# Two sparse-attention stages of a four-layer stack: values as the still operand, output by channel, compressed heads in pairs, spatial weights laid out transposed, a new order of weight pieces

## What is computed

```python
def _nsa(q, k_cmp, v_cmp, k_sel, v_sel, k_win, v_win, gates, pe, w1, w2):
    kc = compress(k_cmp, 0)              # 15 compressed keys and values of 64 channels, 2 groups
    vc = compress(v_cmp, 1)
    p_c = jax.nn.softmax(jnp.where(m_c, s_c, NEG), axis=-1) * m_c
    o_cmp = jnp.einsum('bsghn,bngd->bsghd', p_c.astype(vc.dtype), vc)
    ...                                  # selected branch and window branch: 8 heads, causal
    o = g[..., 0:1] * o_cmp + g[..., 1:2] * o_sel + g[..., 2:3] * o_win

def _gmlp(uv, ln_g, ln_b, ws, bs):
    u, v = jnp.split(jax.nn.gelu(uv), 2, axis=-1)
    v = _layernorm(v, ln_g, ln_b)
    w = ws * jnp.tril(jnp.ones((GM_CHUNK, GM_CHUNK), ws.dtype))
    sv = jnp.einsum('gts,bnsgc->bntgc', w, v) + bs.T[None, None, :, :, None]
    return u * sv.reshape(B, S, GM_WIDTH)

merged = jax.nn.sigmoid(zga) * (y_a @ proj_a[l]) + jax.nn.sigmoid(zgb) * (y_b @ proj_b[l])
h = h + mod[:, 1, 2] * (merged @ w_out[l])
```

## Time and profile before

| | |
|---|---|
| median of 3 runs | 2371.98 us (2371.92 to 2376.93) |
| profiled execution | 2374.35 us, span 2372.5 us, mean granted clock 0.968 |
| PE busy | 2234.7 us (94%) |
| DVE, ACT busy | 1627.3 us (69%), 1067.6 us (45%) |
| first and second sparse stage | about 1340 to 1559 us and 1955 to 2173 us of the span |

### The profile page before, as it was taken

How to read it: one execution, slowest core, us unless ns; L and a number is a source line. 1 busy time by engine, 2 the same in 40 slices (tenths; PEclk the granted TensorE clock), 3 DMA queues, 4 the chain that set the end, 5 groups by cost and what they waited for, 6 DMA issues and landing times.

```text
span 2372.5 us, 29998 instructions
## 1 busy us (share of the span) xinstructions
PE 2234.7 (94%) x10820; PEld 1862.0 (78%) x10820; DVE 1627.3 (69%) x2271; ACT 1067.6 (45%) x1271; POOL 0.2 (0%) x4
## 2 busy tenths in 40 slices
PE   3999999999999987999999998999999999899998
PEld 3887887888788766788788887778878888777887
DVE  5777777877777776776777754577677776447445
ACT  3434524444444554434534545454353455454434
POOL 0000000000000000000000000000000000000000
PEclk9999999999999997999999987899999999789999
DMA  7888524788688442786688642368759875134553
GB/s 307 322 325 291 206 88 160 284 318 316 237 319 314 142 151 98 269 306 246 242 317 318 219 149 73 107 225 329 260 205 335 316 253 188 64 105 139 183 209 125
DMA packets 128374, 537.29 MB, mean 226 GB/s; under 512 B 15040, under 2 KB 15904, under 8 KB 109344
## 3 DMA queue, kind: packets, MB, share of 16 engines
q1 hardware_dynamic: 128288, 536.12, 62.2%
HBM read 534.96 MB, written 1.10 MB: 226 GB/s over the span
## 4 chain that ended last, share of the span: by engine, by line
PE 83%; DVE 9%; ACT 5%; DMA 1%; issue 1%; SPq 0%; ACTq 0%; DVEq 0%
PE GU L1588 14%; PE GU L1592 13%; PE GU L1590 13%; PE PY L1588 11%; PE PY L1592 11%; PE PY L1590 10%; DVE wL L900 3%; ACT wH L513 2%; PE TM L1632 1%; ACT M L565 1%; PE GU L2085 1%; ACT xH L560 1%; PE PY L1995 1%; DMA M<-in_ada_t 1%; PE PY L1898 1%
## 5 line engine op out<-in xcount | busy, mean ns | idle before, releaser
L900 DVE TENSOR_TENSOR wL<-raw,wH 128x2048 fp32r<-128x2048 f32 x344 | 776.8, 2279 | 281.6 <-ACT wH L513 280.0
L513 ACT ACTIVATE wH<-raw 128x2048 fp32r<-128x2048 f32 x344 | 645.5, 1901 | 214.6 <-PE PY L1592 128.9
L1588 PE MATMUL GU<-wH,xH 128*128 128x512 f32 (+1 forms) x1584 | 630.1, 398 | 38.8 <-DVE xL L1024 30.7
L1592 PE MATMUL GU<-wH,xL 128*128 128x512 f32 (+1 forms) x1584 | 617.9, 390 | 0.0
L1590 PE MATMUL GU<-wL,xH 128*128 128x512 f32 (+1 forms) x1584 | 617.1, 390 | 0.0
L1588 PEld LDWEIGHTS GU<-wH,xH 128*128 128x128 f32 x1584 | 299.4, 189 | 106.5 <-issue 27.6
L1592 PEld LDWEIGHTS GU<-wH,xL 128*128 128x128 f32 x1584 | 299.2, 189 | 63.2
L1590 PEld LDWEIGHTS GU<-wL,xH 128*128 128x128 f32 x1584 | 300.0, 189 | 57.6
L913 DVE CUSTOM_DVE_ANT_0 ada<-ada,cond 128x1024 f32<-128x1024 f32 x272 | 316.6, 1221 | 0.0
L593 ACT ACTIVATE hH<-TM 128x512 fp32r<-128x512 f32 x80 | 47.9, 598 | 580.5 <-PE TM L1632 580.5
L1588 PE MATMUL PY<-wH,hH 128*128 128x512 f32 x640 | 198.6, 391 | 0.9 <-DVE wL L900 0.9
(11 more groups left out here) (284 smaller groups left out, 1999.8 us busy)
## 6 DMA issues: line engine op xcount, KB each, us to landing
raw<-in_up_w SPq DMA_DIRECT2D x352, 512.0 KB, 6.3
ada<-in_ada_t SPq DMA_DIRECT2D x136, 1024.0 KB, 7.6
raw<-in_down_w SPq DMA_DIRECT2D x176, 512.0 KB, 5.0
raw<-in_c_w SPq DMA_DIRECT2D x96, 512.0 KB, 4.4
raw<-in_a_w SPq DMA_DIRECT2D x40, 512.0 KB, 4.4
raw<-in_b_w SPq DMA_DIRECT2D x32, 512.0 KB, 4.4
M<-in_ada_t SPq DMA_DIRECT2D x8, 1024.0 KB, 12.4
gB<-gates SPq DMA_DIRECT2D x12, 512.0 KB, 5.6
```

The costliest lines, as they stand in the source:

```text
L513: act.activation(wH[:, to, 0:words], raw[:, slot, 0:words], ACT.Copy).then_inc(s_high, 1)
L900: dve.tensor_tensor(wL[:, to, 0:words], raw[:, slot, 0:words], wH[:, to, 0:words], ALU.subtract).then_inc(s_split, 1)
L1588: pe.matmul(outs[i], aH, wh[i], start=first, stop=False)
L1592: ins = pe.matmul(outs[i], aL, wh[i], start=False, stop=last)
```

## The change

The spatial weights come from the host with the summed token on the partitions, so PE no longer turns them, and both token tiles go through one product: 8 products of 128 columns (L2052) for 16 of 64. Compressed probabilities of two heads stand side by side, 32 columns apart (`pcs`), and are turned together (8 turns of 47 rows, L2059). The compressed values of a group stand twice in `vcb`, on the diagonal, so that one product of 512 columns (L2071) serves four heads and both tiles: 2 products for 16. In the maps the values are the still operand (64 columns) and the probabilities of two heads the moving one (256 columns): 2 products (tile 0) or 4 (tile 1) for 4 or 8 (L2105). The two of a pair write partitions 0 to 63 and 64 to 127 of one bank. The output thus stands by channel, and the turn of `yo_` falls away. The second projection's pieces (18 and 19) now come first, 18 stands in front of the values of map 7; they need the spatial result and not the attention's. `w_out`'s pieces come in the other order of halves. The compressed softmax runs ahead of piece 10 on PE and ahead of piece 12's cut on DVE. Three memsets are new at the start. SP's order is the same.

```diff
@@ pieces
-            + [(k0, C_IN + h * 512, 512) for h in range(2) for k0 in (0, 4)]
-            + [(k0, C_OUT + h * 512, 512) for k0 in (0, 4) for h in range(2)])
+            + [(k0, C_IN + h * 512, 512) for k0 in (4, 0) for h in (1, 0)]
+            + [(k0, C_OUT + h * 512, 512) for k0 in (4, 0) for h in range(2)])
@@ build
+        hcv = sb("hcv", [P, 2, 64])
+        vcb = sb("vcb", [P, 2, P])
+        pcs = sb("pcs", [P, NT * 4 * 64])
@@ scalar, nsa
                 evacuate(u_, GU[:, :, :], ACT.Gelu_apprx_tanh)
-                turned(wsT, TMf)
-                cut()
-                cut()
-                turned(yT, PBf)
+                cut()
                 act.wait_ge(s_cx, t.next(s_cx))
                 act.activation(pcf, pcf, ACT.Exp).then_inc(s_ce, 1)
                 exponentials(0, P)
-                evacuate(sg_[0][:, :, 0:512], PY[:, 0:2, :], ACT.Sigmoid)
-                cut()
-                for i in range(NT):
-                    turned(xn[0:NCMP, i, :], TMf[0:NCMP])
...
+                cut()
+                turned(xn[0:32 + NCMP, 0, :], TMf[0:32 + NCMP])
+                turned(yT, GUf)
...
+                    if u == 6:
+                        act.wait_ge(s_eaten, t.next("done", 2))
+                        act.activation(xH[:, 4:8, :].rearrange("p d s -> p (d s)"), yT, ACT.Copy).then_inc(s_xh, 1)
+                        act.activation(gates_out[u], PY[:, 0:2, :], ACT.Sigmoid).then_inc(s_readA, 1)
...
-                high_out(xH[:, 0:4, :].rearrange("p d s -> p (d s)"), PBf)
...
+                act.wait_ge(s_o, t.next(s_o, 2))
+                act.activation(xH[:, 0:4, :].rearrange("p d s -> p (d s)"), GUf, ACT.Copy).then_inc(s_xh, 1)
@@ vector, nsa
-                for c in range(2):
-                    for i in range(NT):
-                        ins = dve.tensor_scalar(pc_[:, c, 4 * i:4 * i + 4, :],
...
+                        ins = dve.scalar_tensor_tensor(
+                            pc_[:, i, :, c, :],
+                            TM[:, c, 64 * i:64 * i + 64].rearrange("p (m n) -> p m n", n=16)[:, :, 0:NCMP],
+                            0.125, masked(C_CMPN, i, [P, 4, NCMP]), ALU.mult, ALU.add)
@@ tensor, nsa
-                pe.wait_ge(s_wm, t.next(s_wm))
-                pe.wait_ge(s_aT, t.next(s_aT))
-                for g in range(8):
-                    ins = pe.transpose(TMf[:, g * P:(g + 1) * P], ws_[:, g, :], ident)
-                ins.then_inc(s_ot, 1)
...
-                for g in range(8):
-                    for i in range(NT):
-                        ins = pe.matmul(PY[:, 2 + i, g * 64:(g + 1) * 64], wsT[:, g * P:(g + 1) * P],
-                                        vg_[:, i, g * 64:(g + 1) * 64], start=True, stop=True)
...
+                for g in range(8):
+                    ins = pe.matmul(GU[:, g // 4, g % 4 * P:(g % 4 + 1) * P].rearrange("p (t n) -> p t n", t=NT),
+                                    ws_[:, g, :], vg_[:, :, g * 64:(g + 1) * 64], start=True, stop=True)
+                ins.then_inc(s_sv, 1)
                 pe.wait_ge(s_pc, t.next(s_pc))
-                for i in range(NT):
-                    if i:
-                        pe.wait_ge(s_aT, t.next(s_aT))
-                    for h in range(8):
-                        ins = pe.transpose(TMf[0:NCMP, h * P:(h + 1) * P], pc_[:, h % 2, 4 * i + h // 2, :], ident)
-                    ins.then_inc(s_ot, 1)
...
-                for i in range(NT):
-                    for h in range(8):
-                        pe.matmul(GU[:, i, h * 64:(h + 1) * 64], xn[0:NCMP, i, h * P:(h + 1) * P],
-                                  vc_[0:NCMP, h // 4, :], start=(h == 0), stop=False, skip_group_check=True)
+                for h in range(4):
+                    for i in range(NT):
+                        at = (4 * i + h) * 64
+                        ins = pe.transpose(TMf[0:32 + NCMP, h * S + i * P:h * S + (i + 1) * P],
+                                           pcs[:, at:at + 32 + NCMP], ident)
+                ins.then_inc(s_ot, 1)
...
+                def compressed_out():
+                    pe.wait_ge(s_aT, t.next(s_aT))
+                    for g in range(2):
+                        pe.matmul(GU[:, g, :], vcb[0:32 + NCMP, g, :], xn[0:32 + NCMP, 0, g * 512:(g + 1) * 512],
+                                  start=True, stop=False, skip_group_check=True)
...
-                            ins = pe.matmul(GU[:, tile, h * 64:(h + 1) * 64], aT2[u % 2][:, n * P:(n + 1) * P],
-                                            v2_[:, b, k, g * 64:(g + 1) * 64], start=False,
-                                            stop=(b == 1 and k == tile), skip_group_check=True)
+                    weights = aT2[u % 2][:, 0:4 * (tile + 1) * P].rearrange("p (c n k q) -> p c n k q", c=2, n=2, q=P)
+                    for k in range(tile + 1):
+                        for c in range(2):
+                            r = slice(c * 64, (c + 1) * 64)
+                            dst = GU[r, g, :].rearrange("p (n s) -> p n s", n=2)[:, :, tile * P:(tile + 1) * P]
+                            ins = pe.matmul(dst, v2_[:, b, k, g * 64:(g + 1) * 64], weights[:, c, :, k, :],
+                                            start=False, stop=(b == 1 and k == tile), skip_group_check=True)
...
-                turn_tiles(PBf, lambda i, d: yo_[:, i, d * P:(d + 1) * P])
-                pe.wait_ge(s_xl, t.next(s_xl, 2))
...
+                        by_token([PY[:, 0, :], PY[:, 2, :]], 1, tiles=(4, 7))
...
+                by_token([PY[:, 1, :], PY[:, 3, :]], 1, tiles=(4, 7))
+                pe.wait_ge(s_xl, t.next(s_xl))
+                by_token([TM[:, i, :] for i in range(NT)], 0, tiles=(0, 3))
@@ kernel
-    given["gm_ws"] = _np.ascontiguousarray(array("gm_ws_2").transpose(0, 2, 1, 3)).reshape(2, P, D)
+    given["gm_ws"] = _np.ascontiguousarray(array("gm_ws_2").transpose(0, 3, 1, 2)).reshape(2, P, D)
```

More of the change, by code:

```diff
@@ L1525, in nsa @@
-                    cut()
-                t.next(s_readA, 7)
+                    low_out(xL[:, d, :].rearrange("p d s -> p (d s)"), src, xH[:, d, :].rearrange("p d s -> p (d s)"))
+                dve.wait_ge(s_eaten, t.next("done", 13))
+                second(1)
+                low_half(0, GUf)
+                cut()
+                cut()
+                dve.wait_ge(s_eaten, t.next("done", 2))
+                merged(1)
+                dve.wait_ge(s_merged, t.next(s_merged))
+                second(0)
@@ L1528, in out_norm @@
+                low_half(1, TMf)
+                cut()
+                dve.wait_ge(s_eaten, t.next("done", 1))
+                merged(0)
+                cut()
+                low_half(0, TMf)
+                cut()
+                t.next(s_merged)
+                t.next(s_readA, 5)
             def out_norm(tile):
@@ L2046, in nsa @@
                 pairs = lambda u: (u // 2 % 2 * 2, u // 2 % 2 * 2 + 1)
-                pe.wait_ge(s_aT, t.next(s_aT))
-                scores(0, 0, keys(0), pairs(0), qT2, False)
-                by_token(B, 1)
-                pe.wait_ge(s_pc, t.next(s_pc))
-                for i in range(NT):
-                    if i:
-                        pe.wait_ge(s_aT, t.next(s_aT))
-                    for h in range(8):
-                        ins = pe.transpose(TMf[0:NCMP, h * P:(h + 1) * P], pc_[:, h % 2, 4 * i + h // 2, :], ident)
-                    ins.then_inc(s_ot, 1)
@@ L2058, in nsa @@
-                pe.wait_ge(s_readA, t.next(s_readA))
-                pe.wait_ge(s_aT, t.next(s_aT))
-                for i in range(NT):
-                    for h in range(8):
-                        pe.matmul(GU[:, i, h * 64:(h + 1) * 64], xn[0:NCMP, i, h * P:(h + 1) * P],
-                                  vc_[0:NCMP, h // 4, :], start=(h == 0), stop=False, skip_group_check=True)
+                following = lambda u: scores(u, u // 4, keys(u), pairs(u), qT2, False)
+                following(0)
@@ new lines, in nsa @@
+                pe.wait_ge(s_pc, t.next(s_pc))
+                for h in range(4):
+                    for i in range(NT):
+                        at = (4 * i + h) * 64
+                        ins = pe.transpose(TMf[0:32 + NCMP, h * S + i * P:h * S + (i + 1) * P],
+                                           pcs[:, at:at + 32 + NCMP], ident)
+                ins.then_inc(s_ot, 1)
+                slot = t.next("piece") % RING
+                pe.wait_ge(s_split, t.next(s_split))
+                token_tile(B[0], 1, slot, 0)
@@ L2067, in nsa @@
                     if u < 7:
-                        scores(u + 1, (u + 1) // 4, keys(u + 1), pairs(u + 1), qT2, False)
+                        following(u + 1)
+                    if u == 0:
+                        pe.wait_ge(s_aT, t.next(s_aT))
                     pe.wait_ge(s_a, t.next(s_a))
@@ L2088, in nsa @@
                     if u % 4 == 3:
                         ins.then_inc(s_o, 1)
-                pe.wait_ge(s_scored, t.next(s_scored))
```

(13 more changed lines are left out.)

159 lines of the change are left out of this document (77 added, 82 removed).

## The result

The changed kernel takes 2292.6 us (median of four runs, 2291.6 to 2294.5) against 2372.5 us, and the ratio of the two sets of runs is 0.9659 (95% interval 0.9647 to 0.9671): 3.4% faster. The forecast was 2286 with a range of 2279 to 2303; the gain came out as 80 us where 86 were forecast. The profiled run took 2292.84 us, span 2291.1.

The account below looks back on a forecast made before the run. PE, with 83% of the last-ending chain, its waits and half clock were taken as the bound. Savings of 9.9 + 19.3 + 4.3 + 11.7 - 1.6 = 43.6 us, plus 42.5 in the second stage, gave 2286 us, range 2279 to 2303.

Parts of the forecast that it names:

- Spatial products: From the spatial weights' turn to the turn of `y_`: half the products, no layernorm wait; 9.9 us saved, first stage.
- Compressed branch: From its first turn to map 1's products: fewer products and turns at full clock; 19.3 us saved, first stage.
- Values in the maps: Value products in the maps: wider pairs overlapping in two column halves; 4.3 us saved a stage, otherwise 0.9 lost.
- End of the maps: Map 7's turns to the end of piece 18: wait, output turn and half clock go; 11.7 us saved, first stage.
- The new wait: PE ahead of piece 18, waiting for ACT's sigmoid after the copy of `yT`; 1.6 us lost in the first stage.
- Sum: Both stretches, all terms added: 43.6 us saved in the first stage, 42.5 in the second, together 86.1; chance 50%.
- The serial pairs: Rival: column pairs in the maps run one after the other, saving 77.5 us in all, 2294.5; chance 17%.
- Low clock from thin work: Rival: half clock or a late chain stays at one or two places a stage; 2292 to 2303, chance 24%.
- ACT and DVE did not become the bound: Rival denied here: ACT or DVE becomes the maps' bound, 10 to 20 us lost, about 2300 to 2306; chance 6%.

Follow-up runs that it names:

- r3: Changed kernel's order with the spatial, compressed and value products in their old number and size; 2315.2 us, 0.9750 of the kernel before.
- r5: Changed kernel with piece 18 moved behind the values of map 7; 2302.2 us, 0.9699 of the kernel before.
- r6: Kernel before with only the spatial weights laid out transposed by the host, so no turn on PE or copy on ACT; 2378.6 us, ratio 1.0019.
- r2: Changed kernel with both products of each value pair writing the same column half, so they cannot overlap; 2298.8 us, 0.9677 of the kernel before.
- r7: Changed kernel with the sigmoid's table loaded ahead of ACT's wait for piece 17; 2291.3 us, 0.9646 of the kernel before.
- r8: Changed kernel with the last gate's two pieces in swapped order, so ACT copies yT one piece earlier; 2290.2 us, 0.9636 of the kernel before.
- r9: Changed kernel with the 32 compression products split into four groups between halves of pieces, and one ACT cut moved earlier; 2288.8 us, ratio 0.9639.
- r10: Changed kernel with the compression spread in four groups and the last gate's two pieces swapped; 2283.9 us, 0.9626 of the kernel before.
- r12: Changed kernel with compression spread and last gate's pieces swapped, measured again without further edit; 2285.2 us, 0.9621 of the kernel before.

## Why the prediction was right, step by step

The sign, the places and the mechanism held, and the sum nearly so: 80 us came where 86 were forecast. That low clock and waits go is borne out; which of the waits and of the old products had brought the low clock on before is settled only in part (r3 to r5).

*Spatial products.* No wait, 1.78 us for eight (1.85 forecast). In r6 the turn of the weights alone was worth nothing; in r3 the smaller products cost 1.74 more.

*Compressed branch.* 0.85 was worked out for a product of 512 columns from the growth of the scores, 1.7 for two; they take 1.92. The entry and exit that I had set as the upper end are real. The softmax was in time by 1.8 us (done at 1407.3, needed at 1409.07; 1.1 forecast), although the layernorm's last step ended at 1403.1 and not at 1401.6. `y_` was in time by 0.8 us.

*Values in the maps.* The overlap that was assumed from the row pairs is there: 1.02 for two pairs, 0.59 for one, and r2 prices it at 0.43 a pair. My 1.06 and 0.63 were high by 0.04, but 0.09 turned up in the piece ahead, which takes 5.65 from start to start where it took 5.56. The first sentence cited from the Trainium skill, "TensorEngine Tiling (Array Packing)", Key Properties, that tiles work in parallel, agrees for column halves too: 1.02 against 1.87 us.

*End of the maps.* The new wait was forecast as 1.6 us on ACT's sigmoid and is 1.49; r7 takes away the 0.93 of it that stood on the table's place, r8 all of it. r5 shows that the place of piece 18 covers 2.7 us more of ACT's chain.

*Sum.* 43.6 and 42.5 us were forecast for the stretches, 42.5 and 41.4 came. The missing 1.1 us in each is small float32 overhead: 0.2 in the compressed products, 0.3 in piece 11, which takes 2.85 + 2.94 = 5.79 us in its two halves, and about 0.1 in each of the six pieces of the maps.

*What was mis-sized.* 2286 was 6.6 us under the result. 2.2 of it are the two stretches. 2.5 stand outside them, in a term that the sum did not have: the span fell by 81.4 us while the stretches gave 83.9. The second compression, in front of the second stretch, ran at half clock for 10.2 us where it had been 6.8 (442.9 against 441.4 us between the stretches), and the first stretch began at 1386.2 and not at 1385.2. The second is a low stretch of 3.4 us at 296 us of the span that the kernel before had not. The program is the same at both places. r2 had 441.3 again, all other profiles with this compression 442.9 to 443.2, so it can vary and its cause stays open; r9, which takes the low clock away there, is at 438.1. The rest, 2 us, is the base: the sum was taken from a median of 2371.98 of three runs, and the profile that it was worked out on had taken 2374.35; beside the later runs the kernel before had medians of 2373.4 to 2374.9. Taken from that: 2374.35 - 83.9 + 2.5 = 2292.95, against 2292.84 for the profile after.

*Rivals.* The serial pairs fell with r2. Low clock from thin work (small float32 products and turns with no weight piece among them) did not come in the changed kernel, but r3 shows that it was near: with the old compressed products it comes in both stages, without a wait. The rule from the Trainium skill, "TensorE: Matmul & The Clock Gate", Part 4, that turns do not count as busy, did no harm at this density: 1.00 over both stretches, with 4 or 8 turns a map. No run separates turns from other thin work, so whether they count stays open. ACT and DVE did not become the bound; DVE begins to make PE wait where PE comes 5 us earlier (r9, r10).

## What to carry to other kernels

Read the stretch from start to start, take the dense work out of it at its full-clock price, and ask what the rest is. Here waits and half clock were some 32 of 42 us and the instructions themselves about 9, so a piece of independent dense work put where an engine waits was worth more than a smaller instruction count, and removing instructions ahead of a wait gave nothing. A long block of small float32 work can bring the half clock without any wait; where independent dense work is at hand, try breaking the block up with it, as r9 did. And when PE has been made faster, look again at which chain on the other engines ends just in time.

## What the runs showed of the hardware that was not expected

- The clock falls without any idle time. Thirty-two products of 33 columns in a row bring it to 0.50 with PE busy in every microsecond; in groups of eight between dense halves it stays at 1.00 (r9 to r12). Sixteen compressed products of 64 columns did it in r3, in both stages, while sixteen spatial ones of the same width did not. What makes that difference no run shows.
- The same program part ran low for different times: 6.8 us at the first compression and 10.2 at the second of one profile, and 441.3 us between the stretches in one run against 442.9 to 443.2 in the others. A gain below some 2 us in this kernel is to be read from the stretches and not from the total.
- Removing eight turns from PE gained nothing (r6): the wait behind them was longer by 1.2 us and not by the 0.85 of the turns. The kernel came out 0.19% slower, for a reason that isn't shown.
